# Host-laid-out input, parameters and output, and attention scores on half rows of the array, in a two-layer Conformer/attention kernel

## What is computed

```python
for i in range(2):
    h_res = h_res + 0.5 * swiglu(rms_norm(h_res, ffn1_norm[i]), ffn1_w_in[i], ffn1_w_out[i])
    h = rms_norm(h_res, mix_norm[i])
    proj = h @ w_in[i]                       # conv GLU in | q (16 heads of 64) | k, v (4 heads of 64) | gates
    y_a = conv_module(proj[..., :2048], ...) # GLU, causal depthwise conv of 31 taps, layer norm, silu, matmul
    q, k = rms_norm(q, q_norm[i]), rms_norm(k, k_norm[i])
    y_b = window_sink_attention(q, k, v, attn_sinks[i]) @ attn_w_out[i]
    gates = sigmoid(proj[..., o_v:] + gate_bias[i])
    h_res = h_res + (gates[..., :1024] * y_a + gates[..., 1024:] * y_b) @ w_out[i]
    h_res = h_res + 0.5 * swiglu(rms_norm(h_res, ffn2_norm[i]), ffn2_w_in[i], ffn2_w_out[i])
return h_res[:, 16:]
```

## Time and profile before

| | us |
|---|---|
| median of 3 runs (2580.72 to 2587.73) | 2583.41 |
| the profiled execution | 2583.82 |
| its span, first to last instruction | 2582.0 |
| TensorE matmul busy | 2521.7 (98%) |
| TensorE weight load busy | 2345.1 (91%) |
| VectorE busy | 1521.3 (59%) |
| ScalarE busy | 824.5 (32%) |
| GpSimd busy | 757.0 (29%) |

### The profile page before, as it was taken

How to read it: one execution, slowest core, us unless ns; L and a number is a source line. 1 busy time by engine, 2 the same in 40 slices (tenths; PEclk the granted TensorE clock), 3 DMA queues, 4 the chain that set the end, 5 groups by cost and what they waited for, 6 DMA issues and landing times.

```text
span 2582.0 us, 45022 instructions
## 1 busy us (share of the span) xinstructions
PE 2521.7 (98%) x17778; PEld 2345.1 (91%) x17778; DVE 1521.3 (59%) x1628; ACT 824.5 (32%) x1314; POOL 757.0 (29%) x301
## 2 busy tenths in 40 slices
PE   6999999999999999999999999999999999999999
PEld 5999999999999999999999999999878778788887
DVE  5555423799998555554245554248999976555501
ACT  3222222434445232222232222223434443322311
POOL 2444432000003444444334444320000034444443
PEclk9999999999999999999999999999999999999999
DMA  3333332222222323333323333322222223333332
GB/s 96 89 89 89 99 91 80 60 68 59 75 66 69 90 86 91 91 90 94 92 83 90 89 89 96 92 73 68 68 68 74 68 74 98 90 97 90 105 92 87
DMA packets 432906, 216.84 MB, mean 84 GB/s; under 512 B 29770, under 2 KB 431178, under 8 KB 432808
## 3 DMA queue, kind: packets, MB, share of 16 engines
q1 hardware_dynamic: 431648, 215.11, 28.6%
q10 hardware_dynamic: 1160, 0.33, 0.1%
HBM read 212.21 MB, written 2.10 MB: 83 GB/s over the span
## 4 chain that ended last, share of the span: by engine, by line
PE 67%; issue 29%; DVE 2%; ACT 1%; POOL 1%; DMA 0%; ACTq 0%; DVEq 0%; POOLq 0%
PE po L727 66%; POOL wl L422 1%; DMA qkrow<-in_k_norm 0%; ACT cv L686 0%; DVE cv L1297 0%; ACT xh L689 0%; DVE xl L1003 0%; DVE rms L1292 0%; DVE acc_f L1007 0%; DVE xl L1300 0%; ACT wh L457 0%; PE pstat L742 0%; DVE gb L1256 0%; DVE yout L1322 0%; PE po L969 0%
## 5 line engine op out<-in xcount | busy, mean ns | idle before, releaser
L422 POOL TENSOR_TENSOR wl<-raw,wh 128x1024 fp32r<-128x1024 f32 (+1 forms) x292 | 756.1, 2590 | 1803.7 <-ACT wh L457 1803.7
L727 PE MATMUL po<-xh,wh 128*128 128x264 f32 (+1 forms) x3872 | 919.2, 306 | 25.3 <-DVE wl L1177 15.5
L727 PE MATMUL po<-xh,wl 128*128 128x264 f32 (+1 forms) x3872 | 910.0, 304 | 0.0
L727 PE MATMUL po<-xl,wh 128*128 128x264 f32 (+1 forms) x3872 | 909.9, 304 | 0.0
L457 ACT ACTIVATE wh<-raw 128x1024 fp32r<-128x1024 f32 (+1 forms) x376 | 419.1, 1115 | 1434.2 <-PE po L727 1434.2
L727 PEld LDWEIGHTS po<-xh,wh 128*128 128x128 f32 x3872 | 629.2, 191 | 60.8 <-issue 22.0
L727 PEld LDWEIGHTS po<-xh,wl 128*128 128x128 f32 x3872 | 626.1, 190 | 26.2
L727 PEld LDWEIGHTS po<-xl,wh 128*128 128x128 f32 x3872 | 625.4, 190 | 25.7 <-issue 0.2
L1082 DVE SCALAR_TENSOR_TENSOR cv<-ub,lp,cv 128x528 f32<-128x528 f32 (+1 forms) x480 | 344.6, 766 | 1.6
L727 PE MATMUL po<-hh,wl 128*128 128x264 f32 (+1 forms) x1232 | 283.2, 299 | 0.0
L727 PE MATMUL po<-hh,wh 128*128 128x264 f32 (+1 forms) x1232 | 283.0, 299 | 0.0
(11 more groups left out here) (172 smaller groups left out, 1829.7 us busy)
## 6 DMA issues: line engine op xcount, KB each, us to landing
raw<-in_ffn_w_in SPq DMA_DIRECT2D x352, 256.0 KB, 3.1
raw<-in_w_in SPq DMA_DIRECT2D x176, 256.0 KB, 3.3
raw<-in_ffn_w_out SPq DMA_DIRECT2D x64, 384.0 KB, 3.5
raw<-in_ffn_w_out SPq DMA_DIRECT2D x64, 320.0 KB, 3.9
raw<-in_attn_w_out SPq DMA_DIRECT2D x32, 256.0 KB, 3.0
raw<-in_conv_w_out SPq DMA_DIRECT2D x32, 256.0 KB, 3.0
raw<-in_w_out SPq DMA_DIRECT2D x32, 256.0 KB, 3.0
xin<-in_x SPq DMA_DIRECT2D x4, 512.0 KB, 5.6
```

What stands on the lines that cost most here:

```text
L422: nc.gpsimd.tensor_tensor(wl[:, s, 0:k, :], raw[:, s, 0:k, :], wh[:, s, 0:k, :].bitcast(F32), ALU.subtract).then_inc(lo_done, 1)
L727: ins = mm(po[:, 2 * out_slot + h, 0:width], w[:, s, k, :], v[:, k, t:t + width], start=begin and k == 0 and w is wh and v is mh_, stop=la ...
```

## The change

**Host.** `x` (with the meta tokens ahead of it), the parameters, the gains of q and k and the sinks are laid out on the host as the chip holds them, and the output is turned on the host.

**Opening and end.** `resid` is loaded directly, tile by tile, 264 KB each; the parameters in one load of 312 KB; the 49 transposes and the 18 copies fall away. The first weight block is loaded behind tile 1, the second behind tile 7. TensorE's first product waits for the tiles one by one. In the very first norm `stat` stands behind the block. The layer's parameter copies stand behind the first step of the FFN. Each residual tile is written out as it is, when it is done.

**Scores.** `kn` has one plane: the key head in both halves of the partitions, without zeros. Every product takes 64 rows, head 0 on rows 0 to 63 and head 1 on 64 to 127, and the two heads write to different banks of `pstat`.

```diff
+            def load_x(k):
+                sp.dma_start(resid[:, k, :], x[:, k, :]).then_inc(x_in[k], 16)
...
-            ffn_pair(0, 0, B_IN1, ffn1_w_in, 0)
+            load_x(0)
+            load_x(1)
+            square(0, B_IN1, 0, ffn1_w_in, 0)
+            for k in range(2, KD):
+                load_x(k)
+            square(0, B_IN1 + 1, 1, ffn1_w_in, FF)
...
-                            sp.dma_start(kn[HD:P, 1, PAD:], kn[0:HD, 0, PAD:]).then_inc(kn_dup, 16)
+                            sp.dma_start(kn[HD:P, PAD:], kn[0:HD, PAD:]).then_inc(kn_dup, 16)
...
-            for i in range(4):
-                sp.wait_ge(fin_cp, i + 1)
-                sp.dma_start(out[0, i * P:(i + 1) * P, :], yout[:, i, :]).then_inc(fin_out, 16)
+            for m in range(KD):
+                sp.wait_ge(out_taken, tile(LAST, T_OUT2) + m + 3)
+                sp.dma_start(out[:, m, :], resid[:, m, META:]).then_inc(fin_out, 16)
...
+            act.dma_start(prm[:, :, :], params).then_inc(par_in, 16)
+            act.dma_start(qk[:, :], qk_gain).then_inc(par_in, 16)
+            act.dma_start(sink[:, :, :, :], sinks).then_inc(par_in, 16)
...
+            act.wait_ge(par_in, 48)
             for m in range(KD):
-                act.wait_ge(pre_cp, PRE + m + 1)
+                act.wait_ge(x_in[m], 16)
                 x_parts(0, 0, m, m % 2, prm[:, m, R_FFN1 * DEPTH:R_FFN1 * DEPTH + 1])
-                if m < 2:
-                    hi(0, 0, m, KD)
+                if m in (1, 5):
+                    hi(0, 0, m // 4, KD)
...
-                        if i == SB // 2:
-                            for h in range(2):
-                                mm(s_win(i)[:, h, :], q, win[:, h, :], start=True, stop=True)
-                        else:
-                            mm(s_win(i), q, win, start=True, stop=True)
+                        for h, r in enumerate(rows_of):
+                            mm(s_win(i, h), q[r, :], kn[r, c:c + WIN], start=True, stop=True)
+                    for h, r in enumerate(rows_of):
+                        ins = mm(s_meta(i, h), q[r, :], kn[r, PAD:PAD + META], start=True, stop=True)
...
-                    if not lead(l):
-                        nc.vector.memset(s_win(0), NEG)
-                    nc.vector.memset(s_win(1)[:, :, 0:CHUNK], NEG).then_inc(mask_done, 1)
+                    for h in range(2):
+                        if not lead(l):
+                            nc.vector.memset(s_win(0, h), NEG)
+                        nc.vector.memset(s_win(1, h)[:, 0:CHUNK], NEG).then_inc(mask_done, 1)
...
-                nc.vector.memset(kn[:, :, 0:PAD], 0.0)
-                nc.vector.memset(kn[HD:P, 0, PAD:], 0.0)
-                nc.vector.memset(kn[0:HD, 1, PAD:], 0.0)
+                nc.vector.memset(kn[:, 0:PAD], 0.0)
```

More of the change, by code:

```diff
@@ L210, in build, with score, s_win, s_meta @@
         qss = pov[:, 0:2 * NPOS].rearrange("p (n h) -> p n h", h=2)
[L211 to L222, removed]
+        def score(i, h):
+            return pstat[:, h, i * WK:(i + 1) * WK]
+        scr = pstat[:, :, 0:SB * WK].rearrange("p h (i k) -> p h i k", k=WK)
+        def s_win(i, h):
+            a = i * WK + h * META
+            return pstat[:, h, a:a + WIN]
+        def s_meta(i, h):
+            a = i * WK + (1 - h) * WIN
+            return pstat[:, h, a:a + META]
         def drops(l, which):
@@ L542, in attn_exp @@
                     at = (2 * i + h) * WK
[L543 removed]
+                    func(pw[:, (b + 1) % 2, at:at + WK], score(i, h),
                          ACT.Exp, scale=scale, bias=bias, accum_out=psum[:, i, h:h + 1])
@@ L752, in step @@
                     free(l, t_in + 2 * t)
+                    outer = norm(l, which) == 0
                     products(l, n_in + 2 * t, 0, 0, KD, xh, xl, before=x_tile(l, which) if begins else None,
-                             mid=(lambda: stat(l, which)) if begins else None, post=post, late=which == 2)
+                             mid=(lambda: stat(l, which)) if begins and not outer else None, post=post,
+                             late=which == 2)
+                    if begins and outer:
+                        stat(l, which)
                     free(l, t_in + 2 * t + 1)
@@ L1047, in step @@
                     tt(at(hl, t, a), t1[:, a:], at(hh, t, a).bitcast(F32), ALU.subtract).then_inc(h_lo, 1)
-                with dve.Fori(0, KF) as t:
+                step(0)
+                if which == 0:
+                    layer_params(l)
+                with dve.Fori(1, KF) as t:
                     step(t)
@@ L1318, in _, with laid_out @@
                 resid_out(l, B_OUT2, 2, T_OUT2, 3, None)
[L1320 to L1328 removed]
+_INS = ["ffn1_w_in", "ffn1_w_out", "w_in", "conv_w_out", "attn_w_out", "w_out", "ffn2_w_in", "ffn2_w_out"]
+def laid_out(inputs):
+    import numpy as np
+    f = {name: np.asarray(a) for name, a in inputs.items()}
+    tiles = lambda a: np.ascontiguousarray(a.T.reshape(KD, P, a.shape[0]).transpose(1, 0, 2))
+    rows = [f[n] for n in ("ffn1_norm", "mix_norm", "ffn2_norm", "conv_b", "conv_ln_g", "conv_ln_b")]
+    rows += [f["gate_bias"].reshape(2 * DEPTH, D), f["conv_w"].reshape(DEPTH * CONV_K, D)]
+    heads = f["attn_sinks"].reshape(DEPTH, GROUPS, 2, 2).transpose(2, 0, 1, 3)
+    return {
+        "x": tiles(np.concatenate([f["meta_tokens"], f["x"][0]])),
+        "params": tiles(np.concatenate(rows)),
+        "qk_gain": np.ascontiguousarray(np.concatenate([f["q_norm"], f["k_norm"]]).T),
+        "sinks": np.ascontiguousarray(np.tile(heads, (HD, 1, 1, 1))),
+        **{name: np.ascontiguousarray(f[name]) for name in _INS},
+    }
 def kernel(**inputs):
```

166 lines of the change are left out of this document (42 added, 124 removed).

## The result

The changed kernel takes 2550.22 us, the median of 4 runs (2548.74 to 2552.16), where the kernel before took 2583.52 on the same chip (2580.72 to 2587.73). The ratio is 0.9875, 95% interval 0.9862 to 0.9887. The forecast was 2550.0. The profiled execution took 2550.15, its span is 2548.2; the profiled one of before 2583.82 and 2582.0.

What follows compares the result with a forecast made beforehand. TensorE bounds the FFN; both engines are nearly full in the mixer; VectorE's chain behind the parameter loads bounds the opening. Savings 24.0 + 6.6 + 3.2 = 33.8 us from 2583.8 gave 2550.0; range 2544 to 2568.

Steps and rivals of the forecast that it cites:

- the opening: Start to block 1 of the first FFN: block 1 starts at 21.2 instead of 45.6; 24.0 us less overall.
- the scores: Mixer score batches: the two heads' half-row products run in pairs, 0.47 us less per batch, 3.2 us less in all.
- the end: Behind the last residual tile: only one 256 KB write remains, landing after 2.2 us; 6.6 us less.
- P: Opening: time when all three parameter loads have landed, which ScalarE's first rounding needs; taken as 5.5, between 5.0 and 7.5.
- Rival C: Opening: the third parameter load lands late, at 14.2, losing 8.7 us, for 2558.7; chance 0.10.
- The chain of VectorE: Opening: VectorE's splits and sums over eight tiles, 10.4 us plus 3.6 lost beside GpSimd; sum of squares at P + 14.8.
- TensorE's slow start: Opening: TensorE works at half speed at first, covered if it warms as before; otherwise about 3 to 5 us lost.
- The cost of 0.4 ahead of block 2: First FFN: consumers of the later `stat` free block 2's accumulator after 6.1 us, block 1 lasts 5.9; 0.4 with hand-overs.
- the change of form: Score batches: switching the array between full and half-row products costs TensorE 0.15 us at either end.
- B: Score batches: the heads' products run one after the other, 14.2 us more instead of 3.2 less, 2567.4; chance 0.18.
- D: Score batches: half rows cool the array, a lower-clock stretch after each of 24 batches, 82 us, 2632; chance 0.03.
- E: Lower-clock stretches fall elsewhere, as in layer 0's mixer: 7 us at most either way, 2543 to 2557; no chance of its own.

Runs made afterwards that it cites:

- early gate: Changed kernel with ScalarE's first rounding waiting for the large parameter load alone, the q and k gains' product moved behind the first FFN step: 2546.64 us.
- narrow taps with full rows: Changed kernel with full-row scores of before and convolution taps 1 to 30 on 64 columns instead of 528: 2538.51 us, against 2523.85 with half rows.

## Why the prediction was right, and where it was not

**The total** was within 0.2 us, which is partly luck: the opening was 1.6 to 1.8 us dearer than forecast, the scores gave 0.9 to 2.4 us more, the end 0.2 more.

**P.** 6.64, not 5.5, near the upper part of its range of 5.0 to 7.5. The large load landed at 4.87, below the estimate; what set P was the third load, with 8 KB, issued at 1.76 and 4.8 us on its way. I had dismissed the two behind the large one as small, though the earlier trace rows held the warning, a small load with 12.29 us. The early gate gave 1.5 us of it back. Rival C was false: the third load was no later than that.

**The chain of VectorE.** First split P + 0.76 (forecast 0.8). The sum of squares was ready at P + 15.6 and not P + 14.8. The stalls under GpSimd were as forecast: a split of 2.34 and one of 2.45, 3.3 us lost where I had 3.6. What was missing are two waits of 0.58 and 0.37 for ScalarE, which rounds a weight block ahead of tiles 2 and 6 (8.97, 1.04 us). I had summed ScalarE's work and found it shorter than VectorE's chain; it is, but where its two weight blocks stand it is late for a moment, and a chain with no slack pays that. For the stalls the Trainium skill (SBUF — State Buffer, SBUF: two separate sides) gives an exclusive lock that VectorE, with two inputs in on-chip memory, and GpSimd hold against each other for a whole instruction. The trace agrees: a split takes 0.76 alone, and 2.34 if GpSimd's 2.35 us operation has begun 0.58 before it (waiting for its end and then running would be 2.5, an estimate from these rows); with the operation moved to VectorE it costs 1.22.

**TensorE's slow start** was covered, as forecast: products came every 0.22 us from 12.55 to about 18.5, then every 0.12, and the waits of 0.49 and 0.31 for the split behind it show that VectorE and not the array was late. Later experiments show that this depends on the execution: in the profiles of two kernels with the same opening (heads ordered by batch, narrow taps with full rows) TensorE waited 1.9 us for a split at 20.3 or 20.6, the granted clock was 0.50 from 22.3 or 22.4 for 3.4 us, and block 2 started at 30.8 and 31.1 instead of 29.3. The cost of 0.4 ahead of block 2 did not show as a wait; block 1 took 6.04 us where 5.86 stood, so at the start of block 2 (51.46 before, 29.27 after) the opening has given 22.2.

**The end.** 2.0 us from issue to landing of the last write, 2.4 in all to the end of the span; forecast 2.2 and 2.6. With the fixed cost of about 2 us that the Trainium skill (DMA: Bandwidth & Descriptors, Latency and other measured facts) gives, it would have been 2.6 from issue to landing, by the forecast's estimate of the transfer. The trace does not agree: 256 KB, all of it, took 2.0 when nothing else was under way. The median of all eight, beside the weight loads, is 4.2.

**The scores.** Pairs, as forecast, 0.45 us for a chunk; the change of form cost 0.09 us ahead of the first score and 0.08 behind the last and not 0.15 at either end. So a batch counted with both ends, as in the forecast, took 1.54 and not 1.65 (the 1.45 leaves the first end out), and it was 0.58 us shorter and not 0.47. That VectorE swallows batches 0 and 1 and batch 2 arrives was right in mechanism, as the lead in group 1 shows; the size was 0.5 to 0.9 in each group, with 1.1 in the first, where the forecast had 0.47. The mask costs 0.5 us more in all and not 1.2: 24 memsets take 2.9 us by the groups of instructions (busy us, mean ns of one), where 12 took 2.4, since narrower ones are shorter:

```profile
L1106 DVE MEMSET pstat<- 128x64 f32 x16 | 1.6, 112 | 0.4 <-PE pstat L814 0.4
L1105 DVE MEMSET pstat<- 128x128 f32 x8 | 1.3, 165 | 0.7 <-PE pstat L814 0.6
```

**The rivals.** B, heads one after the other, was false: the two instructions of a head that stand in a row, for which I had given it a chance, are within the reach of four. Had the products been written head by head over a batch, more than half of B's price would have come true, 2559.6. D, the cooling, was false for this kernel, but its mechanism exists: in the kernels with full batches of 2.36 and of 2.78 us, four of 24 were followed by a stretch at the lower clock. E was right in kind: between two profiles of the same kernel the stretches differ by 7 us in length.

## What to carry to other kernels

Ask of each saved piece of work who is waited for behind it: here the same scores, 12.3 us less of TensorE's time, were worth 14.7 with VectorE relieved and about 4 with VectorE full, and only those batches arrived behind which VectorE waited for TensorE. Two heads of 64 go side by side on the array's halves if the partners stand at most four instructions apart in the program; ordered by head over a batch they took 2.36 us, more than the 2.12 of the kernel before. A gate on several loads opens with the last of them, however small it is, so let the first consumer wait only for what it reads; and to size a part, compare the same stretch between profiles with the same clock stretches in it, since a difference of two whole profiles carries several us of accident.

## What the runs showed of the hardware

- Products on rows 0 to 63 and 64 to 127, the heads in turn, run as pairs, 6 or 7 ns apart, 0.11 us for a pair; on the same rows 0.11 for each. Partners two or four places apart in the program paired; of twelve against twelve only four did, each with the one four places before it.
- A write of 256 KB with nothing beside it landed 2.0 us after its issue; loads of 1 and 8 KB among the first loads of the kernel took 4.6 and 4.8.
- The lower clock level came behind `head_stats` and behind the long wait in every kernel; in the opening in two profiles, behind a wait of 1.9 us; and behind a batch of scores only in the two kernels whose full batches took 2.36 and 2.78 us, not with 2.12 or 1.45; how long it lasts (3.4 or 6.8 us) differs between executions of one kernel.
- A loop of products that is limited by nothing else runs at 5.840 or 5.873 us for a block for some 250 us on end, by no cause that these runs show.
